# Adding partial sums into the rows on GpSimd instead of VectorE in the second MLP phase

## The reference, cut to what matters

```
h2 = rms_norm(x, w_norm2)
ff = jnp.square(jax.nn.relu(jnp.einsum('bsd,df->bsf', h2, w_ff1)))     # 1152 x 4096
x = x + jnp.einsum('bsf,fd->bsd', ff, w_ff2)                           # 1152 x 1024
```

## Time and profile before

| what | value |
|---|---|
| median of three runs | 2460.8 us (2454.11 to 2462.26) |
| the profiled execution, its own time | 2454.71 us |
| its span | 2452.6 us |
| TensorE busy | 2338.1 us, 95% |
| VectorE busy | 1255.1 us, 51% |
| ScalarE busy | 828.8 us, 34% |
| GpSimd busy | 125.6 us, 5% |
| granted TensorE clock, mean | 0.978 of full speed |

### The profile page before, as it was taken

One profiled execution on the slowest core, in us unless ns is written; L12 is line 12 of the kernel. 1 busy time (PEld: TensorE's weight loads), 2 busy tenths in 40 slices (PEclk: granted clock), 3 DMA queues, 4 the chain that ended last, 5 costly groups with the idle time before them and its releaser, 6 DMA issues. The chain is left out here.

```text
span 2452.6 us, 31662 instructions
## 1 busy us (share of the span) xinstructions
PE 2338.1 (95%) x12710; PEld 2067.5 (84%) x12710; DVE 1255.1 (51%) x2189; ACT 828.8 (34%) x1681; POOL 125.6 (5%) x223
## 2 busy tenths in 40 slices
PE   6999999999999999999999999999999999999997
PEld 6987877999999877777788877789999997777775
DVE  4326865201010297897952478561101014987978
ACT  4123523323232333333431244133323233333333
POOL 4010000000000000000120100010000000000002
PEclk8999999999999999999999999999999999999999
DMA  5111011222223403404120110113322223214032
GB/s 156 43 32 43 19 35 43 90 83 92 92 83 111 148 10 137 146 0 146 26 68 27 31 43 18 48 31 100 100 83 96 88 100 131 95 51 146 17 130 86
DMA packets 154274, 185.47 MB, mean 76 GB/s; under 512 B 9980, under 2 KB 101664, under 8 KB 154128
## 3 DMA queue, kind: packets, MB, share of 16 engines
q1 hardware_dynamic: 150272, 176.16, 21.5%
q0 software_dynamic: 2704, 3.10, 0.6%
q10 hardware_dynamic: 1152, 4.19, 0.4%
HBM read 139.93 MB, written 43.29 MB: 75 GB/s over the span
## 5 line engine op out<-in xcount | busy, mean ns | idle before, releaser
L1471 PE MATMUL ps<-hT_hi,w_hi 128*128 128x384 f32 x1824 | 617.2, 338 | 2.7 <-DVE x L1150 2.7
L1473 PE MATMUL ps<-hT_hi,w_lo 128*128 128x384 f32 x1824 | 615.4, 337 | 0.0
L1472 PE MATMUL ps<-hT_lo,w_hi 128*128 128x384 f32 x1824 | 615.3, 337 | 0.0
L995 DVE TENSOR_TENSOR w_lo<-w_raw,w_hi 128x512 fp32r<-128x512 f32 (+1 forms) x232 | 143.5, 668 | 635.5 <-ACT w_hi L660 635.4
L1471 PE MATMUL ps<-w_hi,f_hi 128*128 128x512 f32 x896 | 360.7, 403 | 36.2 <-DVE f_lo L1235 35.0
L1473 PE MATMUL ps<-w_hi,f_lo 128*128 128x512 f32 x896 | 359.4, 401 | 0.0
L1472 PE MATMUL ps<-w_lo,f_hi 128*128 128x512 f32 x896 | 358.3, 400 | 0.0
L1471 PEld LDWEIGHTS ps<-hT_hi,w_hi 128*128 128x128 f32 x1824 | 344.9, 189 | 3.3 <-DVE x L1150 3.1
L1472 PEld LDWEIGHTS ps<-hT_lo,w_hi 128*128 128x128 f32 x1824 | 344.8, 189 | 0.0
L1473 PEld LDWEIGHTS ps<-hT_hi,w_lo 128*128 128x128 f32 x1824 | 344.7, 189 | 0.0
L1471 PE MATMUL ps<-w_hi,hT_hi 128*128 128x512 f32 (+1 forms) x720 | 278.4, 387 | 8.1 <-ACT vn L849 4.5
(11 more groups left out here) (201 smaller groups left out, 2566.4 us busy)
## 6 DMA issues: line engine op xcount, KB each, us to landing
ff_rows<-q SPq DMA_DIRECT2D x64, 576.0 KB, 2.8
w_raw<-in_w_ff SPq DMA_DIRECT2D x128, 256.0 KB
b<-in_w_ff SPq DMA_DIRECT2D x32, 1024.0 KB, 11.3
a<-ff_rows SPq DMA_DIRECT2D x32, 1024.0 KB, 11.5
w_raw<-in_w_in SPq DMA_DIRECT2D x56, 256.0 KB
w_raw<-in_w_out SPq DMA_DIRECT2D x32, 256.0 KB
out<-xn SPq DMA_DIRECT2D x9, 512.0 KB, 2.6
e_raw<-ff_rows SPq DMA_DIRECT2D x16, 256.0 KB, 9.3
```

What stands on the lines that cost most here:

```text
L995: V.tensor_tensor(wl[:, slot, 0:cols], raw[:, n % RAW, 0:cols], wh[:, slot, 0:cols].bitcast(F32), ALU.subtract).then_inc(w_ready.sem, 1)
L1471: pe.matmul(out, sh, mh, start=first, stop=False)
L1472: pe.matmul(out, sh, ml, start=False, stop=False)
L1473: return pe.matmul(out, sl, mh, start=False, stop=last)
```

## The change

In stages P6 and P7 VectorE now makes the partial sum only (`part[p] = bank + part[p]`). Adding the buffer into the rows of `x` is done by GpSimd, in a new function `part_sums`, with eight instructions a group: four of 128x512 for P6, and four of 128x1024 for P7. A new semaphore `part_added` counts them. VectorE waits for it where it next touches the same rows (P3, P4 and P5 of the next group) or the same buffer (P7), and ScalarE where it fills the buffer anew. GpSimd runs the eight sums of all four groups of a layer before it goes on to `next_powers`, and in the last layer before it loads `gN`.

```diff
+        def part_count(grp, which, p):
+            return (now["l"] * FGROUPS + grp) * 2 * HALF + which * HALF + p + 1
...
+            def part_sums(grp):
+
+                m = grp * len(ORDER)
+                for p in range(HALF):
+
+                    pool.wait_ge(x_added, pair_count(m + 3, p))
+                    xv = x[:, p, 512:1024]
+                    nc.gpsimd.tensor_tensor(xv, part[p][:], xv, ALU.add).then_inc(part_added, 1)
+                for p in range(HALF):
+
+                    pool.wait_ge(x_added, pair_count(m + 5, p))
+                    xv = x[:, HALF + p, :].rearrange("p (n d) -> p n d", n=2)
+                    nc.gpsimd.tensor_tensor(xv, part[p][:].unsqueeze(1).broadcast_to([P, 2, 512]), xv,
+                                            ALU.add).then_inc(part_added, 1)
...
                 powers()
+                for grp in range(FGROUPS):
+                    part_sums(grp)
                 if l == DEPTH - 1:
...
                 if grp > 0:
-                    act.wait_ge(x_added, pair_count(n - 2, p))
+                    act.wait_ge(part_added, part_count(grp - 1, 1, p))
...
                 elif kind == "P5":
 
+                    if grp > 0:
+                        dve.wait_ge(part_added, part_count(grp - 1, 1, p))
...
                 elif kind == "P6":
-                    link(V.tensor_tensor(part[p][:], bank, part[p][:], ALU.add))
-                    ins = V.tensor_tensor(right, part[p][:], right, ALU.add)
+                    ins = V.tensor_tensor(part[p][:], bank, part[p][:], ALU.add)
                 elif kind == "P3":
+
+                    dve.wait_ge(part_added, part_count(grp, 0, p))
                     ins = V.tensor_tensor(right, bank, right, ALU.add)
                 elif kind == "P7":
 
-                    link(V.tensor_tensor(part[p][:], bank, part[p][:], ALU.add))
-                    rows = x[:, HALF + p, :].rearrange("p (n d) -> p n d", n=2)
-                    ins = V.tensor_tensor(rows, part[p][:].unsqueeze(1).broadcast_to([P, 2, 512]), rows, ALU.add)
+                    dve.wait_ge(part_added, part_count(grp, 0, p))
+                    ins = V.tensor_tensor(part[p][:], bank, part[p][:], ALU.add)
                 else:
+
+                    dve.wait_ge(part_added, part_count(grp, 1, p))
                     xv = x[:, HALF + p, 0:512]
                     ins = V.tensor_tensor(xv, bank, xv, ALU.add)
```

More of the change, by code:

```diff
@@ L276, in program @@
         z_hi_done, z_lo_done, z_used = plain("z_hi_done"), plain("z_lo_done"), plain("z_used")
-        part_set = plain("part_set")
+        part_set, part_added = plain("part_set"), plain("part_added")
         s_made, t_made = plain("s_made"), plain("t_made")
```

## The result

The change makes the kernel slower: 2476.86 us (median of 8 runs, 2475.14 to 2492.67) against 2461.59 us (8 runs), a ratio of 1.0068 with a 95% interval of 1.0045 to 1.0092, +16.7 us. The forecast was 2479 us with a range of 2454 to 2505.

The account below looks back on a forecast made before the run. TensorE, busy 95%, was taken to wait at group boundaries on a chain from VectorE's last column sum. Boundaries +4, layer 0's end +7.0 and kernel's end +9.3 made +20 us: 2475 profiled, 2479 by the median, range 2454 to 2505.

Parts of the forecast that it names:

- The hold on VectorE: P6 to P7: while GpSimd adds, VectorE instructions with two SBUF inputs wait the whole sum, 1.2 or 2.4 us; chance 0.76.
- part-hold rival: GpSimd keeps VectorE off for half its time, 0.6 of 1.2 us: -4 us, 2451 to 2456; chance 0.10.
- L1221's end: Group's last column sum: P6 sums +1.9 us, 1.27 shed in P7, net +0.7; six boundaries, +4 us.
- The boundary moves with the end of L1221, one for one: Group boundary: loads wait for the last column sum, so it shifts equally while TensorE has room.
- Low parts for P4: P4's last low part, behind two P7 sums, comes 4.2 us later; TensorE stalls about 4 us more each group.
- Eats the room of 6 us that later goes to the boundary, and is not paid twice: Within a layer, P4's extra stall uses TensorE's estimated 6 us of room per group, adding nothing to the boundary's cost.
- Layer 0's end: The normalisation waits for GpSimd's powers behind its last two P7 sums: +7.0 us, bounds +2.8 and +11.8.
- Kernel's end: The first final row waits for `gN`, loaded by GpSimd after its last sums: +9.3 us, bounds +5.1 and +14.1.
- VectorE is not held: Rival: GpSimd waits and VectorE never does; -23 us, 2432 on the profiled basis, 2437 by the median; chance 0.14.
- The sums are quick: Rival: the hold is full but 128x512 sums take 0.85 us; time +4 us, can't be told apart; no separate chance.

Follow-up runs that it names:

- e3: The changed kernel with the additions of each layer's last group given back to VectorE; ratio 1.0018 to the kernel before.
- e9: The changed kernel plus one GpSimd add of 128x1 per group, ahead of the group's first P6 sum; 2477.27 us in its one run.
- e2: Against the kernel before, only the four P7 additions of a group go to GpSimd, P6 stays on VectorE; ratio 1.0056.
- e11: The same kernel as e2, run again; ratio 1.0041 to the kernel before.
- e4: The kernel before with three of P7's four column sums moved ahead of the stage's operand work; ratio 0.9936.
- e12: The same kernel as e4, run again; ratio 0.9920 to the kernel before.

## Why the prediction was right

The total was right, 2479 against 2476.9 us, and so was the mechanism, the hold and the two ends that pay for it. That it came so close is in part luck: the ends were forecast 4.6 us too large, and the +4 us of the groups came about by another way than their own.

- **The hold on VectorE** was there as said, behind the instruction said. It was taken for the whole of a sum of 1.2 and 2.4 us. It is 1.10 and 2.15 us of sums of 1.67 and 2.33 to 2.88 us (the first sum of a stage holds for less, 0.50 and 1.61): the hold is shorter than the instruction, as the part-hold rival said, and the instruction longer. For the time only the hold counts, and it was within 0.1 and 0.25 us. The Trainium skill's page SBUF — State Buffer, section SBUF: two separate sides, has the lock held for the whole instruction; the trace agrees on the lock, not on its length, since VectorE's 1.10 us of waiting are less than the sum's 1.67 us. The figure of the Trainium skill's page GPSIMD Engine Reference, section Performance versus the Vector engine, scaled to an estimate of 1.1 us for 128x512, fits the hold better than the instruction.
- **L1221's end**: +0.7 us in its group was forecast, -0.4 came. Three holds of 1.10 us and one of 0.5 (the first sum came in while VectorE read PSUM) less 4 x 0.72 are +0.9, less 1.27 shed in P7, -0.4. "The boundary moves with the end of L1221, one for one" held in every kernel (46.7 to 48.1 us from that end to the `z_lo` product), and gives -2 us here. The periods grew by 4.3 all the same, since the clock dropped behind `z_lo` in five of six boundaries, 1.54 us each; the sum had no such term. The forecast of +4 us for this term was right by luck: its own price was some 6 us too high, and the term left out is 7.7.
- **Low parts for P4**: P4's last product comes 2.1 us later in its group, not 4.2, and TensorE's stall there grew by 1.8 us to 2.5, not by 4. Of P6's +1.9 only 0.9 came; of P7's +2.3 it was 1.2, since its first sum held for 1.61 us only and the second for 2.15, less 2 x 1.27. "Eats the room of 6 us that later goes to the boundary, and is not paid twice" held: P4 is later and the wait at P2 vanished, and the stretch to the `z_lo` product is no longer than before. What it left out is that the stall of the boundary then stands at `z_lo`, and that a drop of the clock behind that one is paid. I had loss of clock only for slower sums.
- **Layer 0's end**: +7.0 forecast, +4.8 measured. **Kernel's end**: +9.3 and +6.9. Both are 2.2 to 2.4 us smaller, since the late P4 they rest on is 2.1 us smaller than forecast. The waits are those named. e3's time is about 12 us under that of after, with 5 to 20 by the intervals, and fits the 11.7 of the account.
- **The rivals.** "VectorE is not held" fell with the first row. "Held for part only" had the right kind of hold, but took half of the sum where 0.66 (P6) and 0.75 to 0.92 (P7) were measured, and 1.2 us for a sum of 1.67; its bound (over half is slower) holds. "The sums are quick" fell with 1.67 us.

## What to carry to other kernels

An addition moved from VectorE to GpSimd frees VectorE only as far as GpSimd's reading of SBUF meets PSUM-reading or idle time there: here a sum took 0.72 or 1.27 us off VectorE and held it for up to 1.10 or 2.15. Before work is moved, look at what stands behind it on the new engine at the ends of a phase; two ends cost 12 us here, where six boundaries cost 4. And where loads wait for the last of several instructions, moving those to the front of the queue was worth more (0.992) than moving other work to another engine.

## What the runs showed that was not expected

- The hold goes with what GpSimd reads: 1.10 us for two different 128x512 inputs, 0.85 for two inputs from one buffer, 0.42 for one, none for a memset of 0.53 us. The 0.85 us are of a subtraction and the 1.10 of an addition; no run tells which of the two differences counts.
- GpSimd can wait long for a one-column addition: 3.59 us in all eight groups of e9.
- TensorE's 128x384 matmuls come at two paces at a granted clock of 1.00 and without waits: 579 or 567 in 100 us. e2 had the slow one and e11, the same kernel, the fast; so had e4 and e12. No cause was found.
- A drop of the clock costs by where it falls: behind the wait for `z_lo` 1.5 us of a group (24.4 against 22.9 us), in kernels with and without sums on GpSimd; ahead of it 0.2 us at most, even where it lasts about twice as long (1145 to 1152 us before).
